# Five down blocks of the last feed-forward parts as seven products of halves

## What is computed

```python
    log_i = (ig + b_igate).astype(jnp.float32).transpose(0, 2, 1)
    log_f = jax.nn.log_sigmoid((fg + b_fgate).astype(jnp.float32)).transpose(0, 2, 1)
...
    return jnp.concatenate([attn, hm], axis=-1) @ w_out

def swiglu(h, w_gate, w_up, w_down):
    return (jax.nn.silu(h @ w_gate) * (h @ w_up)) @ w_down
...
        x = x + gt_f[:, None, :] * swiglu(h, w_gate[l], w_up[l], w_down[l])
```

## Time and profile before

| what | us |
|---|---|
| median of 3 runs (2034.15 to 2034.65) | 2034.27 |
| the profiled execution, its own time | 2034.22 |
| its span in the trace | 2032.4 |
| TensorE busy | 2026.5 |
| VectorE busy | 1220.5 |
| GpSimd busy | 1038.9 |
| ScalarE busy | 894.1 |

### The profile page before, as it was taken

One profiled execution on the slowest core, in us unless ns is written; L12 is line 12 of the kernel. 1 busy time (PEld: TensorE's weight loads), 2 busy tenths in 40 slices (PEclk: granted clock), 3 DMA queues, 4 the chain that ended last, 5 costly groups with the idle time before them and its releaser, 6 DMA issues.

```text
span 2032.4 us, 29841 instructions
## 1 busy us (share of the span) xinstructions
PE 2026.5 (100%) x10896; PEld 1712.4 (84%) x10896; DVE 1220.5 (60%) x2142; ACT 894.1 (44%) x1361; POOL 1038.9 (51%) x773
## 2 busy tenths in 40 slices
PE   9999999999999999999999999999999999999999
PEld 7788778889889878877788899898877788989898
DVE  5677335576757637854356767567445478647363
ACT  4124353536446422244445355364446544536352
POOL 5454334476555754443355755556343334656555
PEclk9999999999999999999999999999999999999999
DMA  6332212343543343321233443433221212233233
GB/s 223 107 104 84 83 63 101 117 166 105 187 147 124 104 130 101 104 83 64 82 111 128 142 151 144 166 104 104 97 85 66 80 42 104 84 104 105 104 104 104
DMA packets 37492, 223.99 MB, mean 110 GB/s; under 512 B 6012, under 2 KB 6524, under 8 KB 11744
## 3 DMA queue, kind: packets, MB, share of 16 engines
q1 hardware_dynamic: 31424, 193.48, 27.7%
q10 hardware_dynamic: 5920, 28.55, 4.1%
HBM read 215.59 MB, written 2.10 MB: 107 GB/s over the span
## 4 chain that ended last, share of the span: by engine, by line
PE 98%; DVE 1%; DVEq 0%; issue 0%; ACT 0%; ACTq 0%
PE ps L599 18%; PE ps L601 18%; PE ps L600 18%; PE ps L756 6%; PE ps L758 6%; PE ps L757 6%; PE ps L616 4%; PE ps L617 4%; PE ps L618 4%; PE ps L684 2%; PE ps L648 1%; PE ps L650 1%; PE ps L649 1%; PE ps L705 1%; PE ps L694 1%; PE ps L726 0%
## 5 line engine op out<-in xcount | busy, mean ns | idle before, releaser
L519 POOL TENSOR_TENSOR w_lo<-w_raw,w_hi 128x512 fp32r<-128x512 f32 x544 | 732.0, 1377 | 775.8 <-ACT w_hi L1168 766.5
L1168 ACT ACTIVATE w_hi<-w_raw 128x2048 fp32r<-128x2048 f32 x134 | 256.1, 1911 | 383.5 <-PE ps L601 290.7
L599 PE MATMUL ps<-a_hi,w_hi 128*128 128x512 f32 (+1 forms) x888 | 352.2, 397 | 0.0
L601 PE MATMUL ps<-a_hi,w_lo 128*128 128x512 f32 (+1 forms) x888 | 346.2, 390 | 0.0
L600 PE MATMUL ps<-a_lo,w_hi 128*128 128x512 f32 (+1 forms) x888 | 345.8, 389 | 0.0
L533 POOL TENSOR_TENSOR w_lo<-w_raw,w_hi 128x512 fp32r<-128x512 f32 x164 | 214.6, 1331 | 160.9 <-ACT w_hi L1295 160.9
L599 PE MATMUL ps<-b_hi,w_hi 128*128 128x512 f32 x612 | 238.1, 389 | 0.0
L600 PE MATMUL ps<-b_lo,w_hi 128*128 128x512 f32 x612 | 238.1, 389 | 0.0
L601 PE MATMUL ps<-b_hi,w_lo 128*128 128x512 f32 x612 | 238.1, 389 | 0.0
L599 PEld LDWEIGHTS ps<-a_hi,w_hi 128*128 128x128 f32 (+1 forms) x888 | 165.3, 186 | 48.0 <-issue 9.7
L601 PEld LDWEIGHTS ps<-a_hi,w_lo 128*128 128x128 f32 (+1 forms) x888 | 165.3, 186 | 36.8
(11 more groups left out here) (394 smaller groups left out, 4523.6 us busy)
## 6 DMA issues: line engine op xcount, KB each, us to landing
w_raw<-in_weights SPq DMA_DIRECT2D x176, 1024.0 KB, 4.9
v<-in_ada ACTq DMA_DIRECT2D x24, 1024.0 KB, 4.9
out<-x SPq DMA_DIRECT2D x8, 256.0 KB, 2.5
x<-in_x_in SPq DMA_DIRECT2D x3, 512.0 KB, 6.8
w_raw<-in_weights SPq DMA_DIRECT2D x4, 256.0 KB, 5.5
yc<-in_c_rows ACTq DMA_DIRECT2D x2, 512.0 KB, 3.2
bias<-in_mult_bias ACTq DMA_DIRECT2D x1, 640.0 KB
x<-in_x_in SPq DMA_DIRECT2D x2, 256.0 KB, 4.7
```

Source lines behind the costliest of these rows:

```text
L519: nc.gpsimd.tensor_tensor(w_lo[:, s, piece], w_raw[:, s, piece], f32(w_hi[:, s, piece]), ALU.subtract).then_inc(w_lo_ready, 1)
L599: nc.tensor.matmul(o, wh, hi(kt), start=kt == 0, stop=False)
L601: last = nc.tensor.matmul(o, wl, hi(kt), start=False, stop=kt == depth - 1)
L1168: nc.scalar.activation(w_hi[:, n % 2, :], w_raw[:, n % 2, :], ACT.Copy).then_inc(w_hi_ready, 1)
```

## The change

The second to fourth down block of the second part, and the second and third of the third part, become fast blocks: three with 4 slices in each product and two with 3. Their seven token operands come from h: each up block's two tiles are put in the near and far half of depth (`h_slot`: tile n goes to slot n // 2, plus 4 if n is odd; the rows of w_down are ordered to match), and after every up block of these parts VectorE forms four sums of 256 tokens (`h_forms`), ScalarE writes the high parts of three of them (`h_row_high`), and VectorE the low parts (`h_row_low`). The fourth is split once a part, in `h_last_high` and `h_last_low`. The first down block of each part stays plain, and so does the last of the third part. The weight sums of the second down block, and its first column half, are moved ahead: VectorE makes the sums at the end of the up block's iteration, before the up block's products, and ScalarE writes the column half in that up block's `evict`. The results of a fast down block go straight from the sums into x, the second tile with the sign turned (`minus_gate`, one operation of 128x8).

The gate columns are stored twice, high parts in columns 0 to 35 and again in 64 to 99, where GpSimd replaces them by the low parts in one operation (`split_gates`); a single weight of 100 columns then takes two matmuls a slice (`gate_rows`), one by a_hi and one by a_lo, and VectorE adds the two groups of rows. This adds low weight by low data, which was not computed before. Memory turns 2 and 3 move into attention tile 7, ahead of its last slice, and the tile pair behind it begins with banks 2 and 3. The space for `hs` comes from a smaller DMA scratch area (no GpSimd DMA is used), and the fourth token sum of the input moves to a quarter of a_hi and a_lo that no fast block reads.

```diff
-ROW, FIRST_FREE = 4 * S, 16512
+DMA_SCRATCH = 1024
+ROW, FIRST_FREE = 4 * S, DMA_SCRATCH + 128
...
-FAST = [j for j, kind, *_ in feed_forward() if kind != "down" and j >= C_FF + 5]
+def fast_kind(j, kind, hid, b, nt):
+    if kind == "down":
+        return hid > 0 and 0 < b - nt < (3 if nt == FF_TILES[-1] else 4)
+    return j >= C_FF + 5
+FIRST_DOWNS = [j for j, kind, hid, b, nt in feed_forward() if b == nt and hid > 0]
+H_ROWS = [sum(n // 2 for n in FF_TILES[1:1 + e]) for e in range(len(FF_TILES))]
+FAST = [plan[0] for plan in feed_forward() if fast_kind(*plan)]
...
+        thirteen = ExitStack()
+        hs_all = sb("hs", [P, 2, 2, HK, HS], F32R, thirteen)
+        hs = [hs_all[:, i, :, :, :] for i in range(2)]
+        thirteen.close()
+        hs_raw = sb("hs_raw", [P, 2, 2, HK * HS])
...
+        for place in x_sums:
+            place.append([m[:, 0:HK, HS:S] for m in (a_hi, a_lo)])
+        h_sums = [[[t[:, e, :, :] for e in range(2)] for t in (xs[3], *hs)] + [[m[:, 0:HK, HS:S] for m in place]]
+                  for place in ((b_hi, b_lo), (a_hi, a_lo))]
+        h_sums_f32 = [t.rearrange("p (n t) -> p n t", n=HK) for t in (xs_raw[:, 3, 1, :], hs_raw[:, 0, 1, :], hs_raw[:, 1, 1, :], late_raw[:, :])]
...
+            def split_gates(n, s):
+                pool.wait_ge(w_hi_ready, n - 1)
+                raw, hi = (m[:, s, :].rearrange("p (k c) -> p k c", k=KT)[:, :, LOW_ROW:IF_ROWS] for m in (w_raw, w_hi))
+                nc.gpsimd.tensor_tensor(hi, raw, f32(hi), ALU.subtract).then_inc(w_lo_ready, 4)
...
                     split_fast(n, FAST_BLOCKS.index(n))
+                elif n == LAYERS * LAYER_BLOCKS + C_IF:
+                    split_gates(n, n % 2)
...
-            def fast_block(L, site, k_, j, uses):
...
+            def h_sum_ready(part_, i):
+                if i == 3:
+                    pe.wait_ge(ht_last, part_ + 1)
+                else:
+                    pe.wait_ge(ht_split, H_ROWS[part_ + 1])
             pe.wait_ge(warm_set, 1)
...
+            def gate_rows(t, s):
+                pe.wait_ge(bank_free[t % 4], nth(L, LAYER_BANKS, BANK_USES[t]))
+                pe.wait_ge(w_lo_ready, nth(L, 4 * LAYER_BLOCKS, 4 * C_IF + 3))
+                for kt in range(KT):
+                    for part in (a_hi, a_lo):
+                        last = nc.tensor.matmul(ps[t % 4][0:IF_ROWS, :], wcols(w_hi, s, KT, kt, 0, IF_ROWS), part[:, kt, :],
+                                                start=kt == 0 and part is a_hi, stop=kt == KT - 1 and part is a_lo)
+                last.then_inc(tile_done, 2)
...
-                            tile(L, t, s, KT, 0, a_hi, a_lo, low, m=F_ROW + MH, tiles=2)
+                            gate_rows(t, s)
...
                 if n == 0:
...
             m_turn(1)
+            def last_turns():
+                m_turn(2)
+                m_turn(3)
...
             for n in range(5, KT):
-                attended(n)
-            m_turn(2)
-            m_turn(3)
-            for n in range(4):
-                pe.wait_ge(bank_free[n], nth(L, LAYER_BANKS, BANK_USES[T_OUT + KT + n]))
-            tile_pair([ps[n][:, :] for n in range(4)], (C_OUT + 2) % 2, (a_hi, a_lo),
-                      lambda kt: pe.wait_ge(m_split, kt + 1), lows[2], depth=AT)
+                attended(n, last_turns if n == KT - 1 else None)
+            for kt in range(AT):
+                pe.wait_ge(m_split, kt + 1)
+                lows[2](kt, AT)
+                for n in (2, 3, 0, 1) if kt == 0 else range(4):
+                    if kt == 0:
+                        pe.wait_ge(bank_free[n], nth(L, LAYER_BANKS, BANK_USES[T_OUT + KT + n]))
+                    wh, wl = (wcols(w, (C_OUT + 2) % 2, AT, kt, n * P, P) for w in (w_hi, w_lo))
+                    nc.tensor.matmul(ps[n][:, :], wh, a_hi[:, kt, :], start=kt == 0, stop=False)
...
+                        j += 1
+                        continue
+                    if j in FAST:
+                        fast_block(L, FF, FAST.index(j), j, FAST_USES[j], (b_hi, b_lo), h_sums[part_ - 1], nt // 2,
+                                   lambda i: h_sum_ready(part_ - 1, i))
                         j += 1
...
+                if j not in FIRST_DOWNS:
+                    column_high(f, 0).then_inc(w_hi_ready, 1)
                 if j in FAST:
...
+            def h_row_high(n):
+                act.wait_ge(ht_raw, n + 1)
+                i = n if n < H_ROWS[1] else n - H_ROWS[1]
+                nc.scalar.activation(h_sums[0][0][0][:, i, :], h_sums_f32[0][:, i, :], ACT.Copy)
+                nc.scalar.activation(hs_all[:, :, 0, i, :], hs_raw[:, :, 1, i * HS:(i + 1) * HS], ACT.Copy).then_inc(ht_hi, 1)
+            def h_last_high(part_):
+                deep = FF_TILES[1 + part_] // 2
+                act.wait_ge(ht_split, H_ROWS[1 + part_])
+                nc.scalar.activation(h_sums[part_][3][0][:, 0:deep, :], h_sums_f32[3][:, 0:deep, :], ACT.Copy
+                                     ).then_inc(ht_last_hi, 1)
...
                 act.wait_ge(tile_done, nth(L, LAYER_TILES, t + u))
                 if j + 2 in FAST and u == (j not in FAST):
                     raw_copies(L, FAST.index(j + 2), j + 2)
+                    if j + 1 in FIRST_DOWNS:
+                        column_high(j + 2, 0).then_inc(w_hi_ready, 1)
                 if j == C_FF:
...
-                    nc.scalar.activation(b_hi[:, n - hid, :], g[:, 6 + u, :], ACT.Copy).then_inc(h_hi, 1)
+                    nc.scalar.activation(b_hi[:, h_slot(n - hid), :], g[:, 6 + u, :], ACT.Copy).then_inc(h_hi, 1)
+                    if hid > 0 and u == 1:
+                        h_row_high(H_ROWS[FF_TILES.index(nt, 1) - 1] + (b - 1) // 2)
+                if j in FIRST_DOWNS and u == 1:
+                    h_last_high(FIRST_DOWNS.index(j))
...
-                        nc.vector.tensor_scalar(row, ps[(t - u) % 4][at:at + MH, :], sp[at:at + MH, col:col + 1], None,
-                                                ALU.add).then_inc(bank_free[(t - u + 1 - u) % 4], 1)
+                        gates = ps[(t - u) % 4]
+                        nc.vector.tensor_scalar(row, gates[at:at + MH, :], sp[at:at + MH, col:col + 1], None, ALU.add)
+                        dve.drain()
+                        tt(row, row, gates[LOW_ROW + at:LOW_ROW + at + MH, :], ALU.add
+                           ).then_inc(bank_free[(t - u + 1 - u) % 4], 1)
                         dve.drain().then_inc(f_ready, 1) if u else dve.drain()
...
                 dve.drain().then_inc(gate_scaled, 1)
+            minus_gate = qcol[:, 0, 0:KT]
+            nc.vector.tensor_scalar(minus_gate, mod[:, 5 * KT:6 * KT], -1.0, None, ALU.mult)
...
+                def h_forms(i):
+                    t1, t2, t3, t4 = (m[:, i, :] for m in h_sums_f32)
+                    (near_l, near_r), (far_l, far_r) = ((g[:, 6 + e, 0:HS], g[:, 6 + e, HS:S]) for e in range(2))
+                    tt(t1, near_l, near_r, ALU.subtract)
+                    tt(t3, far_r, near_r, ALU.subtract)
+                    dve.drain()
+                    nc.vector.scalar_tensor_tensor(t2, far_r, -1.0, t1, ALU.mult, ALU.subtract)
+                    dve.drain().then_inc(ht_raw, 1)
+                    nc.vector.scalar_tensor_tensor(t4, far_l, -1.0, t2, ALU.mult, ALU.subtract)
+                def h_row_low(n):
+                    i = n if n < H_ROWS[1] else n - H_ROWS[1]
+                    dve.drain()
+                    dve.wait_ge(ht_hi, n + 1)
+                    hi, lo = (m[:, i, :] for m in h_sums[0][0])
+                    tt(lo, h_sums_f32[0][:, i, :], f32(hi), ALU.subtract)
+                    tt(hs_all[:, :, 1, i, :], hs_raw[:, :, 1, i * HS:(i + 1) * HS], f32(hs_all[:, :, 0, i, :]), ALU.subtract
+                       ).then_inc(ht_split, 1)
+                def h_last_low(part_):
+                    hi, lo = (m[:, 0:nt // 2, :] for m in h_sums[part_][3])
+                    dve.wait_ge(ht_last_hi, part_ + 1)
+                    tt(lo, h_sums_f32[3][:, 0:nt // 2, :], f32(hi), ALU.subtract).then_inc(ht_last, 1)
                 if j == FAST[0] - 3:
                     x_sums_raw()
...
+                if j + 1 in FAST and j not in FIRST_DOWNS:
                     weight_sums(L, FF, FAST.index(j + 1), j + 1)
...
+                if j + 1 in FIRST_DOWNS:
+                    weight_sums(L, FF, FAST.index(j + 2), j + 2)
                 if kind == "up":
...
+                    if hid > 0:
+                        h_forms((b - 1) // 2)
+                        h_row_low(H_ROWS[FF_TILES.index(nt, 1) - 1] + (b - 1) // 2)
                     dve.drain()
                 if kind == "down":
                     for u in range(2):
                         n = 2 * (b - nt) + u
-                        dve.wait_ge(tile_done, nth(L, LAYER_TILES, t + u))
-                        last = nc.vector.scalar_tensor_tensor(x[:, n, :], ps[SECOND_BANKS[t + u]][:, :],
```

(30 more changed lines are left out.)

73 lines of the change are left out of this document (45 added, 28 removed).

## The result

The changed kernel takes **2043.11 us** (median of 6 runs, 2042.39 to 2044.54) against 2034.22 for the kernel before (6 runs, 2033.97 to 2034.65): ratio 1.0044, 95% interval 1.0034 to 1.0054. It is 8.9 us slower; 2040.5 was predicted, with a range of 2035.3 to 2044.0. The profiled execution took 2043.59 us.

The account below looks back on a forecast made before the run. TensorE's matmul stream was taken to bound the kernel: 2034.2 - 3.7 (down blocks) - 1.8 (gate columns) - 0.7 (turns) + 10.3 (handover) + 2.2 (up blocks) = 2040.5 us, range 2035.3 to 2044.0.

Parts of the forecast that it names:

- D1: Second down block after a part's last up block, the first fast one; it starts with a wait for bank 0.
- The handover: From a part's last up block to its first two down blocks: TensorE waits, put at 10.3 us (7.7 to 11.1).
- The walk: Step-by-step chain through ScalarE and VectorE from T to the addition freeing bank 0, T + 13.4; 7.7 us of idle time.
- T: The moment TensorE ends a part's last up block, from which D0 runs.
- Both lengthenings: In the handover: products slowed beside GpSimd (0 to 1.0 us) and late D1 weights (0 to 0.7); 1.3 together, at two places.
- D0: First down block after a part's last up block, plain; its first tile holds bank 0 until VectorE's addition into x.
- The up blocks: Between up blocks VectorE's work exceeds TensorE's 20.16 us; waits of 0 to 3.0 us, taken as 2.2.
- rival C: TensorE's clock also falls behind the handover gaps, adding 1.4 to 5.8 us: around 2043.5 us; chance 0.12.
- The likely case: The forecast itself, without the rivals: 2038 to 2042.7 us; chance 0.60.
- A: Rival: the handover does not wait and only the 6.2 us of savings remain, 2028.0 us; chance 0.12.
- B: Rival: only the bare walk's 7.7 us, no meeting with GpSimd, slack enough in the up blocks: 2035.7 us; chance 0.16.
- D: Rival: some down blocks wait so the seven products gain nothing; ends between B and the forecast; no separate chance.

Follow-up runs that it names:

- old_turns: `plain_downs` with the last two memory turns put back behind tile 7 and the four banks in their old order: 2032.52 us.
- additions_first: The changed kernel with VectorE running D0's two additions into x ahead of the two low parts of D1's weight sums: 2037.15 us.
- sums_unused: `plain_downs` with the token sums of the h tiles made again in the up blocks but read by nothing: 2041.52 us.
- plain_downs: The changed kernel with its five fast down blocks plain again; gate columns, memory turns and new memory layout stay: 2031.79 us.
- filled_gap: The changed kernel with 22 unused matmuls of 256 columns added on TensorE between D0 and D1: 2041.49 us.
- part2_only: The changed kernel with fast down blocks in the second part alone, three of the five: 2036.16 us.
- three_orders: `additions_first` with D1's weight sums behind the low parts of the up block's h tiles, and the last row low part behind D0's additions: 2039.01 us.
- part2_deferred: `part2_only` with D0's additions ahead of the low parts, and the first three up blocks' token sums moved into the following gate block: 2036.67 us.

## Why the prediction was right, and where it was not

**The savings.** Five blocks at 10.08 and 7.56 us (the two D1 but for the slow clock), gate columns 1.8 (1.6 by `old_turns`), turns 0.7 (0.73): all as worked out. By the gap formula of the Trainium skill ("TensorE: Matmul & The Clock Gate", section "Back-to-back issue gap") the blocks would have saved 5.4; it did not apply, as 0.120 us was measured again.

**The handover.** The mechanism and its place were right, and `additions_first` shows that the order of VectorE's program causes it. The walk held in its order, and each step came 0.4 to 0.9 us late. Foreseen from T: weight sums done at 4.25, h tiles split at 7.25, ht_raw at 8.65, D1 at 13.4. Measured in the second part (T = 1892.40): 4.65, 8.15, 9.3 and 14.2; in the third (T = 1999.44) D1 stood at 14.2, too. Both lengthenings that were foreseen are there: the weights landed late for ScalarE's raw copies, which start at T + 0.6 and not T + 0.2 and had waited for the DMA, and the two products took 2.12 instead of 1.51 beside GpSimd. The whole was put at 10.3 and came to 9.1, between the bare 7.7 and the upper bound: the two lengthenings were taken near their upper ends and came out lower. Against the bare walk the wait inside D0 was off most, 1.1 against 1.9; before D1 3.1 and 3.8 were measured, in the forecast's ranges.

**The up blocks.** 2.2 expected, 2.4 measured, in the changed kernel and in `sums_unused`. Three of the four stand at the second product of the following block, as said; the fourth, for GpSimd's low part, stands before a block's first product.

**What failed** is the place of rival C. The forecast had "Full granted clock" and put the fall at 0.12, beside waits of 2.5 to 5 us that it took as nearly certain. It happened at both handovers and cost 3.1 us, inside the 1.4 to 5.8 of rival C, whose 2043.5 is nearer to the measured 2043.11 than the forecast's 2040.5. The likely case ended at 2042.7, below the median; the stated range held it only because it reached over part of C. That no row of before shows a fall was no evidence against one, since no row of before shows such a gap. The chance of C given the waits should have been the larger one. One size in it was off: it took a matmul at 1.2 GHz to last twice as long, and 0.213 against 0.120 was measured, 1.8 times. That 2040.5 + 3.1 hits the profiled execution is partly luck: waits of 11.5 against the 12.5 assumed and the wait at 25.46 nearly cancel.

**The other rivals.** A (no wait) needed the walk 5 us shorter; with the additions in front 1.1 and 1.9 us are still waited before D1, 1.9 inside D0 and 2.7 behind up blocks, more than the 3.7 that the blocks save. B fell with the products beside GpSimd, with the up blocks and with the clock. D came true in part: the two D1, at 11.65 and 9.06 us, lasted longer than the plain 10.90 and 8.17, by the slow clock and not by waits inside them; the other three blocks kept their savings. One sum under "How the numbers follow" is wrong: with the lower ends of both waits the likely case starts at 2034.2 - 6.2 + 7.7 = 2035.7, not at 2038.

**Still open.** The wait of 0.7 us at 25.46 is in the trace of the changed kernel alone. Other traces, of `plain_downs` and the kernel before too, have nothing there; several have a wait of 0.2 to 0.8 us near 7 us instead, for ScalarE. That looks like scatter between executions, but no run isolates it. Why D1's weights landed later in `filled_gap` is not known either. At what gap the clock falls, and why three executions of `part2_only` seem to have kept it, was not looked for.

## What to carry to other kernels

A faster form of a block pays only if its operands are ready: 3.7 us of saved matmuls bought 11.5 us of waits, because the products' operands and the free bank hang on a chain through two engines that the plain form does not have. Price the chain from the end of the producing block, in the order of each engine's program, and expect the clock to fall behind a gap of 2 us or more, as it did in every trace here. Before moving an operation on VectorE, look at what GpSimd does at the new place and what the operation reads.

## What the runs showed of the hardware that was not expected

- In the traces TensorE slowed by 0.09 us a matmul of 256 columns (0.213 against 0.120) and by 0.2 one of 512 (0.43 against 0.227) behind gaps of 2.0 to 3.7 us, for some 11 to 16 matmuls. Where the slowing began differed: with the first matmuls in the changed kernel's third part, 0.9 us after the restart in its second, and 1.4 us after it in `three_orders`. Gaps of 1.0, 1.6 and 1.7 us in `additions_first` and one of 1.7 us in `part2_deferred` had none. By the granted clocks of `part2_only` the same kernel can run with and without a fall.
- VectorE and GpSimd slow each other by what VectorE reads. Beside GpSimd's quarters, operations with both inputs in SBUF took 1.64 (512 columns, usually 0.68) and 1.3 to 1.5 (256 columns, usually 0.43); those with one input in PSUM kept their 0.70. The Trainium skill has this in "SBUF — State Buffer", section "Who interferes with whom": with two SBUF inputs VectorE contends with a reading GpSimd instruction, with one it does not. The traces agree. By it one could have foreseen that `three_orders` and `part2_deferred` would lose; how much is in the traces.
- An idle TensorE can be cheaper filled than left: 22 useless matmuls before the second part's D1 took the place of the idle time, and the granted clock stayed at 1.00 where it was 0.76 without them.
